# An encoder layer: four A pairs of heads ahead of the four B pairs, and P·V as fp32r products of split operands

## The reference

```python
proj = x @ w_in                         # columns: qa ka va qb kb vb
s = q @ k.T * hd ** -0.5 - slope * dist # A: |distance| <= 128, 8 query heads on 2 key heads
p = exp(s - m)                          # A: a sink logit joins the denominator
o = p @ v / p.sum()                     # B: 8 heads; (window, dilation) = (128,1), (512,4), (2048,16),
                                        # branches merged by their softmax denominators
y = concat(rms_norm(oa), rms_norm(ob)) @ w_out
```

## Time and profile before

| | |
|---|---|
| runs | 1449.83, 1456.10, 1455.13 us, median 1455.13 |
| profiled execution | 1452.95 us, span 1451.1 us |
| TensorE matmuls | 1292.6 us (89%) |
| VectorE | 733.5 us (51%) |
| ScalarE | 603.0 us (42%) |
| GpSimd | 123.3 us (8%) |
| x transposed, V projected | 0 to 112 us |
| first groups | 112 to 145 us |
| four passes over the pairs | 145 to 745 us |
| out-projection, router, experts, last norm | 745 to 1451 us |

### The profile page before, as it was taken

One profiled execution on the slowest core, in us unless ns is written; L12 is line 12 of the kernel. 1 busy time (PEld: TensorE's weight loads), 2 busy tenths in 40 slices (PEclk: granted clock), 3 DMA queues, 4 the chain that ended last, 5 costly groups with the idle time before them and its releaser, 6 DMA issues.

```text
span 1451.1 us, 23295 instructions
## 1 busy us (share of the span) xinstructions
PE 1292.6 (89%) x8034; PEld 1165.2 (80%) x8034; DVE 733.5 (51%) x1756; ACT 603.0 (42%) x1440; POOL 123.3 (8%) x172
## 2 busy tenths in 40 slices
PE   6999699979997999899878999988799999999950
PEld 6998588968896889787867888887689999999940
DVE  3111345534554555443647786446456565655354
ACT  3221234433443444333633333231446666666444
POOL 0000000000000000000001211000101111110274
PEclk9999899999999999997569999999799999999985
DMA  5324646264526552646443333013578787885798
GB/s 171 112 80 123 146 126 172 68 169 128 157 67 177 132 153 63 175 132 184 123 153 142 124 139 117 31 57 98 165 274 275 275 273 265 284 265 202 205 238 222
DMA packets 171805, 234.45 MB, mean 162 GB/s; under 512 B 39744, under 2 KB 124736, under 8 KB 171712
## 3 DMA queue, kind: packets, MB, share of 16 engines
q1 hardware_dynamic: 157312, 180.80, 41.7%
q0 software_dynamic: 8064, 29.36, 8.0%
q10 hardware_dynamic: 6336, 23.07, 3.9%
HBM read 141.15 MB, written 59.02 MB: 138 GB/s over the span
## 4 chain that ended last, share of the span: by engine, by line
issue 56%; PE 30%; DMA 6%; ACT 2%; POOL 2%; DVE 2%; DVEq 0%; ACTq 0%; POOLq 0%
PE bank L711 8%; PE bank L713 8%; PE bank L712 8%; PE bank L705 4%; DMA xg<-x_scratch,idc 3%; DMA d_work<-y_scratch,two_i 3%; PE bank L887 2%; POOL d_work L1933 1%; ACT d_work L1292 1%; ACT xgT_hi L1027 1%; DVE xgT_lo L1503 0%; ACT d_work L1360 0%; PE bank L1001 0%; ACT d_work L1354 0%; POOL c_work L1867 0%
## 5 line engine op out<-in xcount | busy, mean ns | idle before, releaser
L1108 ACT ACTIVATE b_work<-b_work 128x256 f32<-128x256 f32 (+3 forms) x288 | 147.9, 514 | 292.8 <-DVE b_work L1440 292.2
L711 PE MATMUL bank<-xgT_hi,w_gu_hi 128*128 128x256 f32 x704 | 204.9, 291 | 7.5 <-DVE xgT_lo L1503 7.5
L712 PE MATMUL bank<-xgT_lo,w_gu_hi 128*128 128x256 f32 x704 | 202.8, 288 | 0.0
L713 PE MATMUL bank<-xgT_hi,w_gu_lo 128*128 128x256 f32 x704 | 202.7, 288 | 0.0
L1449 DVE COPY b_work<-bank 128x256 f32<-128x256 f32 (+2 forms) x256 | 112.7, 440 | 100.7 <-PE bank L786 100.6
L786 PE MATMUL bank<-keep,b_work 128*128 128x128 f32 x608 | 124.1, 293 | 32.5 <-ACT b_work L1108 32.4
L711 PEld LDWEIGHTS bank<-xgT_hi,w_gu_hi 128*128 128x128 f32 x704 | 139.0, 198 | 13.7 <-DVE xgT_lo L1503 8.9
L712 PEld LDWEIGHTS bank<-xgT_lo,w_gu_hi 128*128 128x128 f32 x704 | 139.0, 197 | 0.0
L713 PEld LDWEIGHTS bank<-xgT_hi,w_gu_lo 128*128 128x128 f32 x704 | 138.8, 197 | 0.0
L786 PEld LDWEIGHTS bank<-keep,b_work 128*128 128x128 f32 x608 | 85.2, 148 | 65.1 <-ACT b_work L1108 37.9
L799 PE MATMUL bank<-b_work 128*128 128x64 f32 (+1 forms) x704 | 121.1, 293 | 5.3 <-DVE b_work L1449 5.3
(11 more groups left out here) (186 smaller groups left out, 2851.6 us busy)
## 6 DMA issues: line engine op xcount, KB each, us to landing
y_scratch<-b_work SPq DMA_DIRECT2D x16, 1024.0 KB, 5.2
d_work<-in_w_gate SPq DMA_DIRECT2D x16, 1024.0 KB, 7.3
d_work<-in_w_up SPq DMA_DIRECT2D x16, 1024.0 KB, 9.6
d_work<-in_w_down SPq DMA_DIRECT2D x16, 1024.0 KB, 7.1
y_scratch<-d_work ACTq DMA_DIRECT2D x32, 512.0 KB, 3.1
...
```

What stands on the lines that cost most here:

```text
L711: nc.tensor.matmul(o, w_hi, x_hi, start=first, stop=False)
L712: nc.tensor.matmul(o, w_hi, x_lo, start=False, stop=False)
L713: return nc.tensor.matmul(o, w_lo, x_hi, start=False, stop=last)
L1108: nc.scalar.activation(prob[:, ring(u, last), 0:n], prob[:, ring(u, last), 0:n], ACT.Exp, scale=-1.0, bias=o[:, HD:HD + 1], accum_out=o[:, ...
```

## The change

The four A pairs are worked first, written out, 24 units each; then the B pairs of 48 units, three in a loop and the last written out. Groups are spread as `PLAN_A` to `PLAN_B_LAST` say, each unit mostly with one step; five groups instead of six come ahead of the first unit. Query tiles are now three, one for each third of the tokens (`Q[g]`); B keys and values are held for the short and the long sequence apart; the result buffers are two instead of three. P·V is done with fp32r operands: values are split when they are projected (`v_hi` by ScalarE, low part by VectorE) and stand side by side as 128 columns, so that the scratch `vb_d` is twice as large; ScalarE writes the high part of the transposed probabilities (`pT_high`), VectorE the low part (`pT_low`). The high part is multiplied with both halves of the values, the low part with the high half alone, and VectorE adds the two halves of the sum with a reduction (`results`). TensorE's `pv` comes one unit later. The weights' raw form is loaded into the tile of their low part. Zeroing `y_d` from SBUF is replaced by copies of rows of x from DRAM to DRAM (`fill_y`), all in the A pairs. The output weights are loaded at the start of the last B pair, into the place of a third of x, and split at its units 12 to 39. Memory layouts change accordingly. `wait_copied` waits for the copies of a group by its count.

```diff
-UNITS = 72
+AU, BU = 24, 48
 BLOCK = 8
 GT = 512
-SHORT_UNIT = 48
-PRE = 6
-GROUPS = 9
-LAST_GROUPS = 6
-WO_UNIT = 44
-ZERO_PARTS = 16
-MERGE_UNIT = 62
+SHORT_UNIT = 20
+FILL_PARTS = 16
+MERGE_UNIT = 38
...
-        PROJ = [("q", 2, 0), ("k", 1, None), ("q", 0, 1), ("k", 2, None), ("q", 1, 0), ("q", 2, 1),
-                ("k", 0, None), ("q", 0, 0), ("q", 1, 1)]
-
-        FIRST = [("k", 0), ("k", 1), ("k", 2), ("q", 0), ("k", 0), ("q", 1)]
...
+        def groups_of(pair):
+            i = pair.i
+            if pair.kind == "a" and i < PAIRS - 1:
+                here, there = (w_a, w_b) if i % 2 == 0 else (w_b, w_a)
+                return [(here, 2, "q", i * 3 + 3), (there, 0, "q", i * 3 + 4), (there, 1, "q", i * 3 + 5)]
+            if pair.kind == "a":
+                return [(w_b, 2, "q", 12), (w_a, 0, "k", 4), (w_b, 0, "q", 13), (w_b, 1, "q", 14)]
+            first = [(w_a, 1, "k", i * 3 + 5), (w_a, 2, "k", i * 3 + 6), (w_b, 2, "q", i * 3 + 15)]
+            return first if pair.last else first + [(w_a, 0, "k", i * 3 + 7), (w_b, 0, "q", i * 3 + 16),
+                                                    (w_b, 1, "q", i * 3 + 17)]
+
+
+        FIRST = [(w_b, 0, "k", 1), (w_b, 1, "k", 2), (w_b, 2, "k", 3), (w_a, 0, "q", 1), (w_a, 1, "q", 2)]
...
-        PLAN = proj_plan([(0, 5), (6, 11), (12, 17), (18, 24), (25, 31), (33, 41), (42, 51), (52, 61), (62, 71)])
-        PLAN_LAST = proj_plan([(0, 5), (6, 11), (12, 16), (17, 21), (22, 25), (27, 31)])
...
+        PLAN_A = proj_plan([(0, 7), (8, 15), (16, 23)])
+        PLAN_A_LAST = proj_plan([(0, 4), (5, 10), (12, 17), (18, 23)])
+        PLAN_B = proj_plan([(0, 7), (8, 14), (15, 23), (24, 31), (32, 39), (40, 47)])
+        PLAN_B_LAST = proj_plan([(0, 7), (8, 14), (16, 28)])
...
+        def splits(pair):
+
+            if pair.kind == "a":
+                if pair.i == 0:
+                    return {2: (w_b, 2), 15: (w_a, 3)}
+                return {10 if pair.i == PAIRS - 1 else 15: (w_a if pair.i == 2 else w_b, 3 + pair.i)}
+            return {} if pair.last else {21: (w_a, pair.i * 2 + 7), 30: (w_b, pair.i * 2 + 8)}
...
+        def group_bank(pair, n):
+            return bank[7 - (5 + pair.i * 3 + n) % 2] if pair.kind == "a" else bank[7 - n % 2]
+
+        WO_STEPS = (12, 16, 20, 24, 30, 33, 36, 39)
...
+        def ring(pair, u):
+            return u % 2 if not pair.last or u < SHORT_UNIT else (2, 0, 1)[(u - SHORT_UNIT) % 3]
+
+        def ahead(pair, g):
+
+            if not pair.last or g < SHORT_UNIT - 2:
+                us = [g + 2]
+            elif g == SHORT_UNIT - 2:
+                us = [g + 2, g + 3]
+            else:
+                us = [g + 3]
+            return [at for at in map(pair.at, us) if at is not None]
...
+            def fill_y(n):
+
+                rest = (SLOT_TILES * ST - 2 * TOKENS) // FILL_PARTS
+                first = n * rest % (TOKENS - rest)
+                sp.dma_start(y_d[n * rest + 2 * TOKENS:(n + 1) * rest + 2 * TOKENS, :], x[first:first + rest, :])\
+                  .then_inc(S["y_filled"], 16)
...
+            def a_pair(pair):
+                i, last = pair.i, pair.i == PAIRS - 1
+                groups = groups_of(pair)
+
+                dup(pair.groups - 1, FIRST[4] if i == 0 else groups_of(Pair("a", i - 1))[2])
                 if last:
-                    sp.wait_ge(S["proj_made"], PRE + GROUPS * i + LAST_GROUPS)
+
+                    wait("biased", pair.first)
+                    load_v1(0, V1p, 0, S["v1p_loaded"])
+                    load_v2(0, V2p, 0, S["v2p_loaded"])
+                    sp.dma_start(t1, tab_1[0]).then_inc(S["t1_loaded"], 16)
+                    sp.dma_start(t2, tab_2[0]).then_inc(S["t2_loaded"], 16)
+                elif i > 0:
+                    wait("biased", pair.first)
+                    sp.dma_start(tA[(i + 1) % 2], tab_a[i + 1]).then_inc(S["ta_loaded"], 16)
+                wait("qk_made", pair.first)
+                dup(pair.groups, groups[0])
+                if last:
+                    load_b(w_b, QB0, 0)
+                elif i < PAIRS - 2:
+                    load_qa(groups[0][0], i + 2)
+                else:
+                    load_b(groups[0][0], KB0, 0)
+                fill_y(4 * i)
+                store_o(pair, 0)
+                fill_y(4 * i + 1)
+                wait("qk_made", pair.first + 8)
+                dup(pair.groups + 1, groups[1], KBp if last else None)
+                store_o(pair, 1)
+                fill_y(4 * i + 2)
+                if last:
+                    dup(pair.groups + 2, groups[2])
+                    fill_y(4 * i + 3)
+                else:
+                    fill_y(4 * i + 3)
+                store_o(pair, 2)
...
+            def b_pair(pair):
+                i, last = pair.i, pair.last
+                groups = groups_of(pair)
+
+                dup(pair.groups - 1, (w_b, 1, "q", 0))
+                wait("pv_made", pair.fours)
+                load_v1(i, V1s, 1, S["v1s_loaded"])
+                load_v2(i, V2s, 1, S["v2s_loaded"])
+                if last:
+                    sp.wait_ge(S["proj_made"], pair.groups)
                     for c, part in enumerate((w_out[0:256], w_out[256:512])):
                         sp.dma_start(raw_o[HD * c:HD * c + HD, 0:4, :],
                                      part.rearrange("(i p) n -> p i n", p=HD)).then_inc(S["wo_loaded"], 16)
                     sp.dma_start(raw_o[:, 4:8, :], w_out[512:1024].rearrange("(k p) n -> p k n", p=P))\
                       .then_inc(S["wo_loaded"], 16)
+                wait("qk_made", pair.first)
+                dup(pair.groups, groups[0], KBs[:, :, 0:GT])
+                store_o(pair, 0)
+                dup(pair.groups + 1, groups[1], KBs[:, :, GT:2 * GT])
+                if not last:
+                    load_b(w_a, KB0, i + 1)
+                store_o(pair, 1)
+                dup(pair.groups + 2, groups[2])
+                if last:
                     sp.dma_start(ln1g, ln1_g.partition_broadcast(P)).then_inc(S["wr_loaded"], 16)
                     sp.dma_start(ln1b, ln1_b.partition_broadcast(P)).then_inc(S["wr_loaded"], 16)
-                wait("qk_made", i * UNITS + 40)
-                dup_pair(5, i)
-                store_o(4, i)
-                if last:
-
-                    sp.wait_ge(o_st[0], 16 * 11 + 16)
-                    sp.wait_ge(o_st[1], 16 * 11 + 16)
+                    store_o(pair, 2)
+
+                    sp.wait_ge(S["dup_q"], 128 * groups[2][3])
+                    wait("qk_made", pair.first + 32)
+                    for c in range(2):
+                        sp.wait_ge(o_st[c], 16 * 16 + 16)
                     for t in range(2):
                         sp.dma_start(odt[:, t, :], od_t[t]).then_inc(od_ld[t], 16)
...
+                    for b in range(3, 6):
+                        store_o(pair, b)
+                    return
+                load_b(w_b, QB0, i + 1)
+                wait("pv_made", pair.fours + 4)
+                load_v1(i + 1, V1p, 0, S["v1p_loaded"])
+                load_v2(i + 1, V2p, 0, S["v2p_loaded"])
+                store_o(pair, 2)
+                dup(pair.groups + 3, groups[3], KBp)
+                store_o(pair, 3)
+                dup(pair.groups + 4, groups[4])
+                wait("biased", pair.first + 40)
+                sp.dma_start(t1, tab_1[i + 1]).then_inc(S["t1_loaded"], 16)
+                store_o(pair, 4)
+                wait("biased", pair.first + 48)
+                sp.dma_start(t2, tab_2[i + 1]).then_inc(S["t2_loaded"], 16)
+                store_o(pair, 5)
...
+            def keys_there(pair, u):
+
+                i = pair.i
+                if pair.kind == "a" and i == 0 and u in (0, 8):
+                    wait_copied(pe, "k", 1 if u == 0 else 3)
+                if pair.kind == "a" and u % BLOCK == 0:
+                    wait_copied(pe, "q", i * 3 + (u // BLOCK + 1))
+                if pair.kind == "b" and u in (0, 16, 19):
+                    wait_copied(pe, "k", i * 3 + {0: 4, 16: 5, 19: 6}[u])
+                if pair.kind == "b" and u in (0, 16, 32):
+                    wait_copied(pe, "q", i * 3 + (13 + u // 16))
...
-                o = bank[4 + (u // 4) % 2][:, HD * (u % 4):HD * (u % 4) + HD]
+            def pv(pair, u):
+
+                v = pair.units[u].v
+                if pair.kind == "b" and u in (0, 8, 16, 24):
+                    name, dmas = {0: ("v1p_loaded", 3), 8: ("v2p_loaded", 1),
+                                  16: ("v1s_loaded", 3), 24: ("v2s_loaded", 2)}[u]
+                    pe.wait_ge(S[name], (pair.i + 1) * (16 * dmas))
+                if u % 4 == 0 and not (pair.kind == "a" and pair.i == 0 and u < 8):
+
+                    pe.wait_ge(S["o_ready"], pair.fours + (u // 4 - 1))
+                pe.wait_ge(S["pT_ready"], pair.first + (u + 1))
+                o = bank[4 + (u // 4) % 2][:, P * (u % 4):P * (u % 4) + P]
                 for c, (r, rows) in enumerate(v):
```

(40 more changed lines are left out.)

751 lines of the change are left out of this document (361 added, 390 removed).

## The result

The kernel after takes 1506.2 us as the median of four runs (1499.7 to 1512.3), the one before 1453.1 (1449.8 to 1456.1). The ratio is 1.0365, with a 95% interval of 1.0309 to 1.0421: slower by 3.7%, and 3 us outside the forecast's range. The profiled execution took 1509.6 us, with a span of 1507.7.

A forecast was written before the change was run, and what follows sets the result against it. TensorE's own work was taken to set the heads stage's pace: 509.2 us of work plus 93.6 of waits made 602.8 against 600. With the rest carried over, the forecast was 1458 us, range 1422 to 1503.

The forecast's parts named there:

- P·V costs nothing: TensorE's P·V: old and new forms both go at the pace of two weight loads a block, priced at nothing.
- The rival that the fp32 form is bound by its streaming: P·V: the fp32 records' 0.11 us is streaming, so the change takes 85 us off, 1373; chance 0.07.
- The sum of the work: TensorE's work in the heads stage, A and B pairs without waits: 509.2 us.
- The key copy before unit 19: B pairs 0 to 2: TensorE idles 3.6 us for the second key group's copy, plus 1.4 us of low clock.
- w_out's cost: Last B pair: ScalarE waits for w_out in unit 12 and blocks all exponentials, 14 us, plus 2 of slow clock.
- The copy from DRAM to DRAM: A pairs: the 1 MB copy x to y lands in the 5.2 us of the old zero store.
- the 8 us at which the forecast called itself wrong: A pairs: the forecast is wrong if the copies to y land after 8 us.
- The third rival: A pairs: the DRAM-to-DRAM copy pays read after write, 10.4 us instead of 5.2; 43 us slower, 1501; chance 0.13.
- The store of block 2: B pairs 0 to 2: store behind the value loads, 1.5 us each; last pair, behind two ln loads, 2.7.
- The slow clock: TensorE after waits: 1.4 us behind each key wait in B pairs 0 to 2; last pair's units 29 to 47, 12.
- The jumps: B pairs: two jumps back to a loop's start, 2.4 us each as before, 4.8 in all.
- The second rival: Stage's waits overlap or transfers land sooner, in w_out, key waits and tail: some 25 us off, 1433; chance 0.20.

The follow-up runs named there:

- moves_and_fill: all_moves with the fills of y read from a constant SBUF tile and the last A pair's weight split in unit 11: 1415.6 us, ratio 0.9754.
- all_moves: Kernel after with store_first, plan_early and store_second together, and w_out loaded in three pieces behind small transfers, split in units 31 to 38: 1422.4 us, ratio 0.9793.
- pv_fp32: Kernel after with each block's P·V as one fp32 matmul of the high part with 64 value columns: 1500.1 us, ratio 1.0345.
- pv_high: Kernel after with P·V's low-part matmul left out, only the 128-column fp32r matmul kept: 1468.4 us, ratio 1.0107.
- splits_late: Kernel after with w_out loaded where it was but split in units 29 to 38 instead of from unit 12: 1505.3 us, ratio 1.0386.
- plan_early: Kernel after with the B pairs' first three projection groups in earlier units (0-5, 6-11, 12-23): 1466.9 us, ratio 1.0125.
- sbuf_fill: Kernel after with the 16 fills of y read from a constant SBUF tile, in pieces of 256 numbers, instead of x in DRAM: 1497.7 us, ratio 1.0324.
- store_second: Kernel after with block 2's store issued ahead of the next pair's loads in B pairs 0 to 2: 1484.2 us, ratio 1.0225.
- store_first: Kernel after with the first block's store issued ahead of the first copy to y in the A pairs: 1486.1 us, ratio 1.0231.

## Why the prediction was wrong

The forecast's stage runs from 145 us to the transposes of the out-projection, which start at 796.16 in the kernel after: 651.2 us against 602.8. By its terms:

| term | forecast | measured | in |
|---|---|---|---|
| first units | 5 | 3.1 | after: first score at 148.09, less 145 |
| an A pair's bare work | 45.4 | 47.0, waits under 2 us in it | moves_and_fill |
| A pairs 0 to 2 beyond 136.2 | 6.6 | 27.4 | after |
| last A pair | 56.3 | 57.1 | after |
| a B pair's bare work | 84.7 | 84.05 | all_moves |
| B pairs 0 to 2 beyond 254.1 | 24.3 | 38.4 | after |
| last B pair beyond 67.9 | 52.4 | 66.9 | after: 134.8 to the transposes |

The part behind the stage, carried over at 706.7 us, took 711.5.

**P·V costs nothing** (right). 0.12 us a record, and pv_fp32 and pv_high bear it out. The rival that the fp32 form is bound by its streaming, by which the change would have won 85 us (its own numbers, 0.22 less 0.09, make it 80), is ruled out for 64 columns: pv_fp32 is no slower. The Trainium skill counts four passes for true FP32 ("FP8 and Floating Point Precision", TensorE Precision Notes); no run here counts passes, but with 64 columns they don't set the time. The rule of the Trainium skill on LDWEIGHTS in "TensorE: Matmul & The Clock Gate", columns/1.2 ns, gives an estimate of 107 ns for 128 columns, and the 0.105 us of pv_high agrees.

**The sum of the work** (right to 1 or 2 us a pair). It was counted from unit starts, and with the waits gone that is what a pair takes.

**The places of the waits** (right but for one, which no term names). The key copy before unit 19 (3.3 us against 3.6), the last query group (7.8 against 8.2), the weights in the last A pair (2.8), the store in the A pairs and w_out are all there. The one is in the last pair: w_out's cost, 14 us, has the right size in part by luck. I let it hold ScalarE, which it did (13.7 us), and forgot what is queued behind it on SyncE, the first key group's copy, which held TensorE at the same time and 1.1 us longer. splits_late shows that TensorE waits about as long without ScalarE's wait for w_out, and plan_early that with an earlier plan even ScalarE waits for this copy.

**The copy from DRAM to DRAM** (mis-sized). I took 5.2 us from the old fills; it was 8.8, which is also over the 8 us at which the forecast called itself wrong. The third rival has the direction right, though not its 10.4 and not shown in its reason, a read paid after a write: sbuf_fill puts 2.3 of the 3.6 us on the source and its pieces, and leaves 1.3 unexplained. The copy did what the rival says to the store, 5.1 us of TensorE's idle time a pair; the delay of the next pair's Q1, the other 21 us of that rival, didn't come.

**The store of block 2** (mis-sized). 1.5 us for the store behind the value loads in B pairs 0 to 2 was taken without working out when it lands. VectorE waited 4.5 to 4.9 us and TensorE 3.3 to 3.7, and store_second gives back some 6 a pair. The same store in the last pair, behind the two ln loads, was priced at 2.7 and held TensorE for 5.5.

**The slow clock** (mis-sized, and the largest term). I gave the key wait 1.4 us of it, from one row that was followed by matmuls of 0.50 us, and the waits for stores none. In the kernel after the key wait of 3.3 us costs some 7 (plan_early), the store's 3.4 some 6 (store_second) and the first A pair's 5.4 cost 6.9 (store_first). Of the 132.7 us beyond the bare work (27.4 + 38.4 + 66.9), waits of 2 us or more are 73.7 (15.3, 20.3, 38.1), and 59 are slow clock and short waits, by subtraction; the forecast had 61 of the first and 22 of the second. So 37 of the 48 us that the stage missed are there, some 5 of them bare work of the A pairs. The trace of before would have told more than its one row. Behind that 3.96 us wait it has 0.83 and 0.75:

```profile
653.00:663.00 10.00, 9.13 (x42) 7.39 (x43) 3.19 (x12) 2.66 (x10) 0.00 (x0) 0.83 0.46 105
663.00:680.00 17.00, 16.64 (x80) 14.35 (x78) 8.12 (x39) 7.71 (x28) 0.00 (x0) 0.75 0.65 160
```

and each of its four passes has a wait of 4.8 to 6.9 us behind ScalarE's wait for a weight load, with the clock at 0.75 to 0.80 over the next ten us, so 2.0 to 2.4 us lost each. One of them, and the stretch behind it:

```profile
322.09 0.90 PE L786 MATMUL bank<-keep,b_work 128*128 128x128 f32 x3 [6.60 <-ACT b_work L1108]
322.09:332.00 9.91, 9.91 (x54) 8.95 (x55) 4.29 (x13) 3.17 (x10) 0.00 (x0) 0.77 0.82 203
```

Another slip is too small to matter: the last A pair's weights land at 9 + 5.3 = 14.3 us by the forecast's own numbers, not at 13.6.

**The jumps** (wrong, small). I carried over 4.8 us for two jumps back to the loop's start; no wait stands at a B pair's start now (units there take 1.61 and 2.05 us).

**The second rival,** that waits overlap and transfers land sooner, was given 0.20 and was wrong in every part. The range ended 3 us too low because two of its terms stood at one end of what the rows allowed with no bound of their own: the clock behind a wait, and the store behind the value loads. The first of them is the step that failed: the key wait's clock priced at 1.4 us and that of the store waits at nothing, where the runs show some 4 and some 2.5.
